# Second block's output norms: mean on all partitions by a constant stationary matrix, root and reciprocal on full rows, the last output job as two jobs

## What is computed

```
def rmsnorm(x, g):
    y = x * lax.rsqrt(jnp.mean(x * x, axis=-1, keepdims=True) + RMS_EPS)
    return y * g

for l in range(2):
    h = rmsnorm(x, norm_mix_pre[l])
    ... three branches, gated: merged
    x = x + rmsnorm(merged @ w_out[l], norm_mix_post[l])          # p1
    h = rmsnorm(x, norm_mem_pre[l])
    ... attention to 256 memory rows
    x = x + rmsnorm(attended @ w_mo[l], norm_mem_post[l])         # p2
    h = rmsnorm(x, norm_ffn_pre[l])
    ... up projection, convolution over time, gate
    x = x + rmsnorm(y @ w_down[l], norm_ffn_post[l])              # p3
```

## Time and profile before

| | |
|---|---|
| median of 3 runs | 1674.55 us (1674.32 to 1675.46) |
| the profiled execution | 1677.06 us |
| its span, first to last instruction | 1675.3 us |
| PE busy | 1633.7 us, 98% of the span |
| DVE busy | 1201.9 us, 72% |
| ACT busy | 899.0 us, 54% |
| POOL busy | 114.6 us, 7% |
| mean granted PE clock | 0.995 of full |

### The profile page before, as it was taken

The page is one execution under the profiler, slowest core; times in us unless marked ns, Lnnn a source line. Parts: engine busy times, 40 slices in busy tenths (PEclk is TensorE's granted clock), DMA queues, the critical chain, the costliest instruction groups (busy, mean ns, idle before and its releaser), DMA issues.

```text
span 1675.3 us, 31896 instructions
## 1 busy us (share of the span) xinstructions
PE 1633.7 (98%) x13590; PEld 1576.9 (94%) x13590; DVE 1201.9 (72%) x1781; ACT 899.0 (54%) x1374; POOL 114.6 (7%) x72
## 2 busy tenths in 40 slices
PE   9988999999999999999999999999999999999997
PEld 9977999999879999989899989999899999999997
DVE  5887777656976776477859758983667768579863
ACT  5585644454676444544545755544535546655542
POOL 2020000020110000210000110001200001110000
PEclk9999999999999999999999999999999999999999
DMA  8313555553225655555345335554454455345550
GB/s 291 108 65 107 198 194 194 178 192 129 95 71 194 208 187 197 204 187 172 131 170 182 127 132 193 204 187 165 159 169 170 143 175 174 122 149 208 199 184 34
DMA packets 52830, 274.31 MB, mean 164 GB/s; under 512 B 6096, under 2 KB 6736, under 8 KB 52560
## 3 DMA queue, kind: packets, MB, share of 16 engines
q1 hardware_dynamic: 52544, 271.22, 47.3%
q10 hardware_dynamic: 144, 1.05, 0.2%
HBM read 271.19 MB, written 1.05 MB: 163 GB/s over the span
## 4 chain that ended last, share of the span: by engine, by line
PE 74%; DVE 17%; ACT 5%; issue 3%; DMA 0%; POOL 0%; SPq 0%; ACTq 0%; DVEq 0%; POOLq 0%
PE bank L795 16%; PE bank L798 15%; PE bank L797 15%; DVE weights_lo L660 4%; PE scores L795 3%; PE scores L798 3%; PE scores L797 3%; PE heads L795 2%; PE heads L798 2%; PE heads L797 2%; ACT weights_hi L649 2%; DVE x_lo L942 1%; ACT probs L1213 1%; DVE x L2410 1%; DVE y L2408 1%
## 5 line engine op out<-in xcount | busy, mean ns | idle before, releaser
L660 DVE TENSOR_TENSOR weights_lo<-raw,weights_hi 128x1536 fp32r<-128x1536 f32 (+2 forms) x344 | 583.8, 1715 | 228.7 <-ACT weights_hi L649 228.3
L649 ACT ACTIVATE weights_hi<-raw 128x1536 fp32r<-128x1536 f32 (+4 forms) x352 | 499.7, 1440 | 178.6 <-PE bank L798 78.6
L795 PE MATMUL bank<-x_hi,weights_lo 128*128 128x256 f32 (+1 forms) x1588 | 447.3, 282 | 2.6 <-DVE gates L2483 1.7
L798 PE MATMUL bank<-x_hi,weights_hi 128*128 128x256 f32 (+1 forms) x1588 | 440.7, 278 | 0.0
L797 PE MATMUL bank<-x_lo,weights_hi 128*128 128x256 f32 (+1 forms) x1588 | 440.7, 278 | 0.0
L795 PEld LDWEIGHTS bank<-x_hi,weights_lo 128*128 128x128 f32 (+1 forms) x1588 | 297.3, 187 | 8.4 <-issue 4.1
L797 PEld LDWEIGHTS bank<-x_lo,weights_hi 128*128 128x128 f32 (+1 forms) x1588 | 296.8, 187 | 2.0 <-issue 2.0
L798 PEld LDWEIGHTS bank<-x_hi,weights_hi 128*128 128x128 f32 (+1 forms) x1588 | 296.9, 187 | 0.0
L795 PE MATMUL bank<-hidden_hi,weights_lo 128*128 128x256 f32 x692 | 191.5, 277 | 0.4 <-DVE hidden_lo L2262 0.4
L797 PE MATMUL bank<-hidden_lo,weights_hi 128*128 128x256 f32 x692 | 191.1, 276 | 0.0
L798 PE MATMUL bank<-hidden_hi,weights_hi 128*128 128x256 f32 x692 | 191.1, 276 | 0.0
(11 more groups left out here) (431 smaller groups left out, 3414.5 us busy)
## 6 DMA issues: line engine op xcount, KB each, us to landing
raw<-in_w_b SPq DMA_DIRECT2D x194, 768.0 KB, 4.2
raw<-in_w_a SPq DMA_DIRECT2D x120, 768.0 KB, 4.3
raw<-in_w_a SPq DMA_DIRECT2D x16, 512.0 KB, 3.6
raw<-in_w_b SPq DMA_DIRECT2D x10, 512.0 KB, 4.0
raw<-in_w_b SPq DMA_DIRECT2D x2, 752.0 KB, 4.1
raw<-in_w_a SPq DMA_DIRECT2D x2, 736.0 KB, 8.4
raw<-in_w_b SPq DMA_DIRECT2D x2, 720.0 KB, 4.6
raw<-in_w_a SPq DMA_DIRECT2D x2, 672.0 KB, 7.1
```

The lines of the kernel that those rows point to most:

```text
L649: nc.scalar.activation(whi[c % SPLIT][:, 0:n], raw[c % RAW][:, 0:n], ACT.Copy).then_inc(*s.mark("weights_hi", c))
L660: nc.vector.tensor_tensor(wlo[c % SPLIT][:, 0:n], raw[c % RAW][:, 0:n], whi[c % SPLIT][:, 0:n].bitcast(F32), ALU.subtract).then_inc(*s.mar ...
L795: ins = nc.tensor.matmul(dst, wl, xh, start=start, stop=False, skip_group_check=skip)
L798: ins = nc.tensor.matmul(dst, wh, xh, start=False, stop=stop, skip_group_check=skip)
```

## The change

The column sums become a mean that stands on all partitions at once. `QUIET[:, 1:2]` is set to 1/1024, and PE uses it, broadcast to 128x128, as the stationary operand; the squares are the moving operand, 256 columns. Three such matmuls accumulate in one bank: POOL's sum (row 0 of `SQ`), the square of the seventh tile (row 6) and that of the eighth (row 7), so DVE adds no squares any more in p1, p2 and p3. The root runs on 128x256 from PSUM into `T2`, the reciprocal on 128x256 from `T2` into `T1`, and DVE multiplies `Y` by `T1`. The spread and its bank are gone from the second block.

The last job of `out`, `mo` and `down` becomes two jobs of one tile each (`out3`/`out4` and so on); the splits of weights that went with the last job go with the first of the two. The fillers are 2 before the mean, none at the spread, and 9 instead of 7 before `ua0` and `q0`. The norms n1, n2 and n3 at the head of each part stay as they are.

```diff
@@ second_jobs @@
-    for i in range(4):
-        job(f"out{i}", "w_out_2", "merged", cols(i * T, 2), full)
+    for i in range(5):
+        job(f"out{i}", "w_out_2", "merged", cols(i * T, 2) if i < 3 else cols((i + 3) * P, 1), full)
...
@@ transformer @@
-        WAITS = {"p1_sum": 3, "p1_factor": 3, "p2_sum": 7, "p2_factor": 3, "ua0": 7, "p3_sum": 7, "p3_factor": 3, "q0": 7}
+        WAITS = {"p1_sum": 2, "p2_sum": 2, "ua0": 9, "p3_sum": 2, "q0": 9}
...
@@ scalar_root @@
-            nc.scalar.activation(NROOT[:, 0:4], pl.bank(f"{tag}_sum")[:, 0:4], ACT.Sqrt, scale=1.0 / DM, bias=eps_col)\
+            nc.scalar.activation(T2[:, 0:T], pl.bank(f"{tag}_sum")[:, 0:T], ACT.Sqrt, bias=eps_col)\
...
@@ vector_norm_sum, now vector_norm_factor @@
-            nc.vector.reciprocal(NFACT[:, 0:4], NROOT[:, 0:4]).then_inc(*s.mark("norm_factor", tag))
+            nc.vector.reciprocal(T1[:, 0:T], T2[:, 0:T]).then_inc(*s.mark("norm_factor", tag))
...
@@ tensor_norm @@
+            mean = QUIET[:, 1:2].to_broadcast([P, P])
             keep_busy(ps, WAITS[f"{tag}_sum"])
-            pe.wait_ge(*s.at(l, "sq_sum", tag))
-            for m in range(QT):
-                ins = nc.tensor.matmul(ps[:, 2 * m:2 * m + 2], SQ[:, 0, m * P:(m + 1) * P], ones[:, 0:2], start=True, stop=True)
+            for n, (row, what) in enumerate(((0, ("sq_first", tag)), (6, square_mark(tag, 3)), (7, square_mark(tag, 4)))):
+                pe.wait_ge(*s.at(l, *what))
+                ins = nc.tensor.matmul(ps[:, 0:T], mean, SQ[:, row, :], start=(n == 0), stop=(n == 2), skip_group_check=True)
...
@@ tensor_b @@
-                elif kind == "spread":
-                    tensor_spread(pl, pe, l, name)
...
@@ scalar_y @@
-            nc.scalar.activation(SQ[:, 2 * i:2 * i + 2, :], two(ps[:, :]), ACT.Square).then_inc(*s.mark("y_sq", name))
-            for k in range(2):
-                ins = nc.scalar.activation(Y[:, 2 * i + k, :], ps[:, k * T:(k + 1) * T], ACT.Copy, scale=gain_b(g, 2 * i + k))
+            tiles = (2 * i, 2 * i + 1) if i < 3 else (3 + i,)
+            n = len(tiles)
+            nc.scalar.activation(SQ[:, tiles[0]:tiles[0] + n, :], ps[:, 0:n * T].rearrange("p (a n) -> p a n", a=n), ACT.Square).then_inc(*s.mark("y_sq", name))
+            for k, tile in enumerate(tiles):
+                ins = nc.scalar.activation(Y[:, tile, :], ps[:, k * T:(k + 1) * T], ACT.Copy, scale=gain_b(g, tile))
...
@@ vector_post @@
-            dve.wait_ge(*s.at(l, "filled", f"{tag}_factor"))
-            factor = pl.bank(f"{tag}_factor")[:, 0:T].rearrange("p (a n) -> p a n", a=1)
+            dve.wait_ge(*s.at(l, "norm_factor", tag))
+            dve.wait_ge(*s.at(l, "y_scaled", {"p1": "out4", "p2": "mo4", "p3": "down4"}[tag]))
+            factor = T1[:, 0:T].rearrange("p (a n) -> p a n", a=1)
...
@@ block.vector @@
-            nc.vector.memset(QUIET[:, :], 0.0)
+            nc.vector.memset(QUIET[:, 0:1], 0.0)
+            nc.vector.memset(QUIET[:, 1:2], 1.0 / DM)
```

More of the change, by code:

```diff
@@ L276, in second_jobs @@
     job("mv", "w_mkv_2", "mem", [[(MW, MW)]], full, feature=False)
-    for i in range(4):
-        job(f"mo{i}", "w_mo_2", "memo", cols(i * T, 2), even(MEM_H))
+    for i in range(5):
+        job(f"mo{i}", "w_mo_2", "memo", cols(i * T, 2) if i < 3 else cols((i + 3) * P, 1), even(MEM_H))
     for i in range(KF2 // 2):
@@ L281, in second_jobs @@
         job(f"ub{i}", "w_up_2", "x3", cols(FF2 + i * T, 2), full)
-    for i in range(4):
-        job(f"down{i}", "w_down_2", "h", cols(i * T, 2), even(KF2))
+    for i in range(5):
+        job(f"down{i}", "w_down_2", "h", cols(i * T, 2) if i < 3 else cols((i + 3) * P, 1), even(KF2))
     return jobs
@@ L1800, in transformer @@
         order_b += [("job", "out0"), ("mem_split", 0), ("job", "out1"), ("mem_split", 1), ("job", "out2"), ("root_table", "out"),
-                    ("job", "out3"), ("job", "mk0a"), ("mem_keys", "mk0a"), ("norm", "p1"), ("spread", "p1"), ("job", "mk0b")]
+                    ("job", "out3"), ("job", "out4"), ("job", "mk0a"), ("mem_keys", "mk0a"), ("norm", "p1"), ("spread", "p1"), ("job", "mk0b")]
         order_b += [("front", ("n2", i)) for i in range(4)] + [("squares", "n2"), ("mem_keys", "mk0b"), ("job", "mq0"), ("adds", "n2"), ("job", "mk1"), ("mean", "n2"),
@@ L1805, in transformer @@
                     ("mem_turn", 2), ("mem_turn", 3)] + [("mem_values", h) for h in range(MEM_H)]
-        order_b += [("root_table", "mo")] + [("job", f"mo{i}") for i in range(4)] + [("norm", "p2"), ("spread", "p2")]
+        order_b += [("root_table", "mo")] + [("job", f"mo{i}") for i in range(5)] + [("norm", "p2"), ("spread", "p2")]
         order_b += [("front", ("n3", i)) for i in range(4)] + [("squares", "n3"),
@@ L1818, in transformer @@
         order_b += [("ffn_in", n), ("ffn_taps", n), ("chunks", (done + 1, done + 1)), ("ffn_out", n), ("ffn_lo", n)]
-        order_b += [("job", "down0"), ("root_table", "down")] + [("job", f"down{i}") for i in range(1, 4)] + [("norm", "p3"), ("spread", "p3")]
+        order_b += [("job", "down0"), ("root_table", "down")] + [("job", f"down{i}") for i in range(1, 5)] + [("norm", "p3"), ("spread", "p3")]
         PRE = {"n1": "norm_mix_pre_2", "n2": "norm_mem_pre_2", "n3": "norm_ffn_pre_2"}
-        own_splits = {"mk0a", "mk0b"} | {f"{u}{i}" for i in range(1, KF2 // 2) for u in ("ua", "ub")} - {"ua1"}
+        whole = {"out3": "out4", "mo3": "mo4", "down3": "down4"}
+        own_splits = set(whole.values()) | {"mk0a", "mk0b"} | {f"{u}{i}" for i in range(1, KF2 // 2) for u in ("ua", "ub")} - {"ua1"}
         QK_B = [j for i in range(3) for j in (f"q{i}", f"k{i}")]
@@ L2315, in scalar_b @@
                     if name not in own_splits:
-                        split_hi(pl, act, l, pl.last_chunk(name) + (3 if name in ("out1", "out2", "out3") else 2))
+                        split_hi(pl, act, l, pl.last_chunk(whole.get(name, name)) + (3 if name in ("out1", "out2", "out3") else 2))
                     if name == "v0":
@@ L2417, in vector_b @@
             for kind, name in order_b:
-                if kind == "adds" or kind == "norm" and ("adds", name) not in order_b:
+                if kind == "adds":
                     vector_adds(pl, dve, l, name)
@@ L2422, in vector_b @@
                 if kind == "norm":
-                    vector_norm_sum(pl, dve, l, name)
+                    vector_norm_factor(pl, dve, l, name)
                 elif kind == "merge_lo":
```

5 lines of the change are left out of this document (2 added, 3 removed).

## The result

The changed kernel takes 1679.65 us (median of 8 runs, 1678.78 to 1686.94). The kernel before, run in turn with it, takes 1674.61 (8 runs, 1673.43 to 1675.46). The medians differ by 5.0 us (0.30%). The ratio is 1.0036, 95% interval 1.0024 to 1.0047, which is slower by more than the 0.2% that can be told from no change. This ratio is not that of the two medians, which is 1.0030; read as a time it is 6.0 us and not 5.0. The forecast was 1681.1 (1677.3 to 1686.0), slower by 6.5. The profiled execution took 1679.84, with a span of 1678.0 and a mean granted clock of 0.992.

The account below looks back on a forecast made before the run. The kernel was taken as a long run of TensorE products, movable only where PE waits: six norms. p1 costs 3.8 us, p2 and p3 2.8, together +6.5 on the median 1674.55: 1681.1 us, range 1677.3 to 1686.0.

Parts of the forecast that it names:

- reciprocal, 256 columns: DVE's full-row reciprocal in p1, p2 and p3, extrapolated at 6.3 ns a column from narrower rows: 1.77 us.
- root, 256 columns: ACT's full-row root after the mean, taken from the four-column root plus 0.9 ns a column: 0.48 us.
- mean, six records: PE's three fp32 matmuls that sum the squares on every partition, priced from the memory scores: 1.52 us.
- p1, later by: Norm after the out jobs, both layers: first multiply of Y comes 1.84 us later, DVE's adds having been partly hidden.
- p2 and p3, later by: Norms after mo and down, both layers: first multiply of Y comes 0.64 us later, at 989.22 instead of 988.58.
- six places: Norms p1, p2 and p3 in two layers, each timed from before its filler to Y's first multiply; together 6.24 us longer.
- multiply of a pair: DVE's multiplies of Y read the factor from SBUF instead of PSUM: 12 ns more each, 0.05 us a norm.
- the steeper rival: Reciprocal grows faster beyond 32 columns, 7.9 ns a column, 2.12 us each: +8.6 us, 1683.2; chance 0.13.
- Everything passes on: After each norm's first multiply nothing has slack, so its delay moves the following job, mk1 or ub0, in full.
- p1 hidden: Rival: mk1 is set by something other than x_lo, so p1's 3.8 us go: +2.8 us, 1677.3; chance 0.06.
- The clock: Rival: PE idles before ua0 and its clock falls, at both p2 and the first p3: up to +4.8 us; chance 0.20.
- The sum against the profiled execution: The whole kernel's +6.5 us added to the profiled execution of 1677.06 us: 1683.6 us.

Follow-up runs that it names:

- e1: The changed kernel with its 256-column reciprocal replaced by a copy of the same size; 1670.80 us, ratio 0.9989 to the kernel before.
- e4: The changed kernel with norm p1 alone put back in its old form (DVE adds, four-column root and reciprocal, spread); 1678.04 us, ratio 1.0028 to the kernel before.
- e4_again: The changed kernel with norm p1 alone in its old form, run a second time on another chip; 1678.45 us, ratio 1.0016 to the kernel before.
- e2: The changed kernel with 17 fillers instead of 9 before ua0 and q0; 1680.47 us, ratio 1.0041 to the kernel before.
- e0_after: The changed kernel run again without any edit; 1679.06 us, ratio 1.0038 to the kernel before.
- e10: The kernel before with split last jobs and, in p2 and p3, narrow sums on PE ordered by operand arrival; 1670.78 us, ratio 0.9958.
- e5: The kernel before with split last jobs and PE summing squares, root and reciprocal still on four columns; 1674.80 us, ratio 0.9989.
- b_again: The kernel before, unedited, run once more against itself; 1678.32 us, ratio 1.0007.
- e0_again: The changed kernel, unedited, run once more on another chip; 1680.57 us, ratio 1.0013 to the kernel before.
- e3: The kernel before with only the last job of out, mo and down split in two; 1673.10 us, ratio 0.9979.
- e9: The kernel before with narrow sums of squares on PE and the last job left whole; 1673.45 us, ratio 0.9983.
- e11: The changed kernel with its last jobs whole again instead of split; 1681.66 us, ratio 1.0019 to the kernel before.

## Why the prediction was right, step by step

**Each new term, forecast and measured.**

| term | forecast | measured |
|---|---|---|
| reciprocal, 256 columns | 1.77 (1.63 to 1.88) | 1.753 |
| root, 256 columns | 0.48 (0.37 to 0.48) | 0.474 |
| mean, six records | 1.52 | 1.46 |
| filler, four records | 0.45 | 0.45 |
| p1, later by | 1.84 | 1.75 |
| p2 and p3, later by | 0.64 | 0.55 (p3 of layer 0: 0.75) |
| six places | 6.24 | 5.90 |
| multiply of a pair | 679 + 12 ns | 685 |

The two terms by slope decided, and they held. The line through the rows from 4 to 32 columns led within 1% of the time of a row eight times as wide, and what the slopes of its two halves gave (1.63 and 1.88) lies on either side. The Trainium skill (VectorE: DVE Perf Modes, the walkthrough of the 8-slice pipeline) gives the reciprocal a repeat count of 8, from which the estimate was 2.3 us; the trace has 1.753, so the measurement stands below the estimate, and the steeper rival fell.

**What was mis-sized.** The mean block came 0.06 cheaper: (1.46 - 0.38) / 5 = 0.216 a record, where I had 0.226 from the memory scores. The row had been misread. In the memory scores, too, the records start 0.216 apart, all but the first, which holds the engine for 0.30; the average over the group's seven steps spread that over all of them. The group's mean of 389 ns fits: one record of 462 and seven of 379. The multiplies cost about 0.03 a norm and not 0.05. With the reciprocal and the root that makes 0.09 in each place. By places and multiplies the change is 5.9 + 0.2 = 6.1 us; the three ratios give 4.9 in the mean and the medians 4.0. The 1 to 2 us between lie within the scatter of the chips (1.8 to 5.2) and were not settled.

**One step was wrong in p3 of layer 0.** I wrote that nothing is lost there because POOL is ready at about the filler's end. POOL, PE and PE's weight loads in the changed kernel:

```profile
1177.90 0.73 POOL L856 TENSOR_TENSOR squares<-squares 128x256 f32<-128x256 f32 x1
...
1178.14 0.60 PE L721 MATMUL bank<-quiet 128*128 128x128 f32 x4
1178.68 1.56 PE L888 MATMUL bank<-squares,quiet 128*128 128x256 f32 x6
...
1178.68 1.16 PEld L888 LDWEIGHTS bank<-squares,quiet 128*128 128x128 f32 x6
...
987.11 1.17 PEld L888 LDWEIGHTS bank<-squares,quiet 128*128 128x128 f32 x6
```

POOL ends at 1178.63, and the mean starts at 1178.68 instead of 0.45 after the filler's start, at 1178.59; it then takes 1.56 and not 1.46. The weight loads show why. The wait for POOL stands ahead of the first one, so it starts only at 1178.68, together with its matmul. At p2 of layer 0 (last line) it had started at 987.11, beside the filler and 0.11 ahead of the matmul at 987.22. So with a wait of 0.09 the weight load is no longer hidden either, which accounts for the other 0.10, and the place is 0.2 longer than the others. A cover of nothing should have been priced from both sides.

**Everything passes on.** Multiplies start later by 1.87 and 2.43 at the first two places, 3.20 at the third, 5.00, 5.59 at the next two, and 2.76 at the last, behind the fast stretch. In layer 0 mk1 and ub0 start later by what their multiply does (1.88 and 1.87; 2.46 and 2.43). e1 gives back 8.3 us of 8.7. So "p1 hidden" falls by the trace; the times of e4 and e4_again alone would not have settled it.

**The clock.** The rival was right in what happens and wrong in what it costs. I priced the low clock as if PE had had work to do. It only follows x_hi there, and ub0 waits for DVE as it did before; e2 removed the fall without gaining anything. At the first p3, the third place that I counted, the clock stayed up in this profile. It did not in e0_after, the same kernel, which has falls after p2 and p3 of layer 0 and after p1 of layer 1, and none after the second p2, though PE idles 1.90 us there too:

```profile
1188.00:1189.00 1.00, 0.83 (x4) 0.86 (x5) 0.96 (x3) 0.58 (x3) 0.00 (x0) 0.50 0.00 0
```

In both profiles the way from the multiply to the next job is 10.64 to 10.65 us at both p2 and at p3 of layer 0, and 10.03 to 10.06 at both p1, with a fall or without. So nothing hangs on which places were hit.

**The sum against the profiled execution did not hold.** I set the +6.5 against a profiled time of 1677.06 and expected 1683.6 for a profiled execution of the changed kernel; it took 1679.84. The places moved by 5.9 and the multiplies by 0.2, the span by 2.7. The rest, 3.4, is the pace of the products, which differs between executions of one kernel: between e0_after and this profile, the same kernel twice, the stretch from 1520 to 1602 alone differs by 3.1 us. Two windows of the kernel before and two of the changed one, in the FFN of layer 1, columns as above; the number in brackets after PE's busy time is the count of its records:

```profile
1570.00:1580.00 10.00, 10.00 (x87) 10.00 (x86) 9.03 (x12) 5.41 (x7) 0.00 (x0) 1.00 0.69 225
1590.00:1600.00 10.00, 10.00 (x87) 10.00 (x87) 7.55 (x10) 4.61 (x6) 0.00 (x0) 1.00 0.62 204
```

```profile
1575.00:1585.00 10.00, 10.00 (x91) 10.00 (x90) 9.82 (x14) 6.03 (x8) 0.00 (x0) 1.00 0.69 221
1595.00:1605.00 10.00, 10.00 (x90) 10.00 (x90) 7.52 (x13) 4.94 (x6) 0.00 (x0) 1.00 0.51 175
```

PE is never idle, the granted clock is 1.00, the instructions are the same, and yet ten microseconds hold 87 records in the one and 90 or 91 in the other (those that reach in over an edge included). That is how the changed kernel caught up 3.4 us there. The +6.5 could not be read from a difference of two profiled spans; the forecast was put on the median of the runs, and that was right.

## What to carry to other kernels

A reciprocal is priced by its columns: put it where the row is narrow, even if a matmul is needed to spread its result, and take the price by width from rows that are already in the trace before moving it. Adding on PE by accumulation was a gain where the operands were ordered by when they come (e10) and waited where they were not (e5), and a filler that goes may uncover a wait for another engine, here POOL. Compare small changes by the length of the places that they touch; the kernel before alone had medians from 1673.90 to 1678.77 on five chips, as much as this whole effect of 0.3%. And a fall of the clock is to be priced by whether PE has work under it.

## What the runs showed of the hardware that I had not expected

**Two paces of TensorE at full clock.** Products of 256 columns in fp32r start 113 ns apart in some stretches and 116 to 118 ns apart in others, some of them as long as the 80 us from 1520 to 1602, at a granted clock of 1.00 in both. Which stretches are slow differs between executions of one kernel. Over the 10,248 products of the three lines the mean at full clock is 114.57 ns in the kernel before, 114.74 in b_again, 114.26 in the changed kernel, 114.80 in e0_after and 114.58 in e0_again; 0.1 ns is 1.0 us of span. Brought to one pace, the spans of the changed kernel are 1681.2, 1681.4 and 1679.6, those of the kernel before 1675.3 and 1675.4: a difference of 5.4, near the 5.9 of the places, and good to about 1 us because of what comes next. What sets the pace was not found and stays open; both paces occur in the stretch from 1520 to 1602 in profiles of one kernel (changed: fast, e0_after and e0_again: slow). But both profiles of the kernel before have it slow, and those of e1, e2, e3, e5, e9, e10 and e11 fast; with so few profiles it isn't shown that an edit can't move the pace.

**A fall of the clock costs nothing in one place and its full price in another.** After p2 in both layers of the changed kernel's first profile the granted clock is 0.50 for about three us, after 1.90 us of idling and then thin work; taking it away left the time where it was (e2). At 385 us, far from the change, a fall meets a PE without a gap. It is long in the kernel before and in the changed kernel, and half as long in e0_after and e0_again. The kernel before, then e0_again:

```profile
389.00:391.00 2.00, 2.00 (x11) 2.00 (x11) 1.97 (x4) 0.00 (x0) 0.00 (x0) 0.50 0.19 25
```

```profile
389.00:391.00 2.00, 2.00 (x19) 2.00 (x18) 1.93 (x4) 0.00 (x0) 0.00 (x0) 1.00 0.42 95
```

Over the products between 369 and 496 e0_again is 1.65 us shorter than the kernel before, and e0_after 1.6. That is the 1.6 us of a fall that the prediction had used, measured, and a second source of scatter between profiles of one kernel, beside the pace.

**The reciprocal by width.** 163 ns for 1 column, 177 for 4, 245 for 16, 354 for 32, and now 1753 for 256: (1753 - 354) / 224 = 6.25 ns a column from 32 on, beside 0.294 us for a copy of the same 256 columns and 0.42 for an add. The cost grows in a straight line, and at no width measured here does it stream as an add does.
